# Weight splits, transposes and a third unit's values moved in the attention parts of a two-layer decoder trunk

## The chip, the cores and the metric

One Trainium2 chip, one core. The metric is device time in microseconds (us) of one execution; the kernel before takes 1085.67 us, the median of three runs (1085.3 to 1085.98).

## The reference

Two layers over 256 tokens of width 1024. Each layer is a half-step feed-forward block, a token mixer, a cross attention over 256 memory rows, and a second half-step feed-forward block, each between two root-mean-square normalisations:

```
for l in range(2):
    x = x + 0.5 * rmsnorm(swiglu(rmsnorm(x, g0), ffn[l, 0]), g1)
    h = rmsnorm(x, g2)
    if l == 0:   # four heads of causal attention (MLA) beside four heads of mLSTM
        y = concat(mla(h), mlstm(h)) @ ab_w_out
    else:        # sparse attention, keys chosen by an indexer
        y = dsa(h) @ c_w_out
    x = x + rmsnorm(y, g3)
    x = x + rmsnorm(cross_attention(rmsnorm(x, g4), rmsnorm(mem)), g5)
    x = x + 0.5 * rmsnorm(swiglu(rmsnorm(x, g6), ffn[l, 1]), g7)
```

The mLSTM part of the first mixer takes queries, keys and values of four heads, gates `li` and `lf = log_sigmoid(f)`, and works in two chunks of 128 tokens. Within a chunk the decay matrix is `cumsum(lf)` differences plus `li` under a causal mask; `sc = q k^T * exp(dmat - m)`; the first chunk's state is `sum(exp(g - m_new) k v)`; the numerator over the denominator is then normalised over each head's 128 values, multiplied by a gain, added to a skip term and gated with `sigmoid(og)`.

## The kernel before

It is written engine by engine, each with its own list of instructions in a fixed order, and semaphores between them. There is no planner: the order of each list is the schedule, and an instruction that waits holds everything behind it on its engine.

**Weights.** All large weights come as chunks of 1 MB (128 x 2048 fp32). SyncE loads a chunk into one of two or three raw slots. ScalarE writes its rounded half into a ring of four (`hi_half`, line 1656, "the high split"); VectorE writes the remainder (`lo_half`, line 2322, "the low split"); then the raw slot is free for the next load. Chunks for the memory keys and values (names `xk`, `xv`) are scaled by a gain on the way, in eight pieces (lines 1652 and 2316). TensorE forms each product from three terms, high x high, high x low, low x high. `split_to(c)` on either engine means: do your half of all chunks up to `c`, here. The chunks of the first mixer's output projection are `abo.0` to `abo.3`. `hi_half` and `lo_half` take the chunks strictly in order.

**PSUM.** Four banks rotate among all intermediate results in one fixed list (`bank_uses`): a result takes a bank when the result four places ahead in the list has been read (`take`). The other four banks hold the output rows `y`.

**First mixer, the order on TensorE.** mLSTM queries and keys (`mq`, `mk`), transposed values (`vmT`), transposed rotary parts (`rT`), the gate product `gT` (line 1427), attention scores of units 0 and 1 (lines 1267 and 1270), `gates`, the transposed keys `ktok`, half of the output gate's projection `og.0` (lines 784 to 786), transposed probabilities `pT0`, `pT1`, the running sum `cum` of the log gates (line 1298), scores 2 and 3, the decay rows `arow.0` and `arow.1`, `og.1`, `pv0`, `pv1` (attention times values, line 1289), the mLSTM scores `S.0`, `S.1`, `pT2`, `pT3`, `state.0`, `state.1`, `pv2`, `pv3`, transposed scaled scores `scT.0`, `scT.1`, `qc`, the numerators `num`, output rows from `abo.0` and half of `abo.1` (line 1076), the transposed normalised heads `hnT.0`, `hnT.1` (line 1153), and the rest of the output rows.

**First mixer, VectorE and ScalarE.** VectorE makes masked scores and row maxima (lines 2559 and 2562), ScalarE the exponentials (line 1824), VectorE the normalised probabilities (line 2574). VectorE scales the skip term `xcT` (line 2168), makes `lf` (line 2170), reads the decay rows (line 2189), reduces them (line 2191), subtracts the row maxima (line 2200), evacuates attention outputs (`output_lo`, line 2583, after ScalarE's `output_hi`, line 1839), forms the exponents `ex` (lines 2212 to 2214) that ScalarE exponentiates at line 2010, and scales the scores into `sc` (line 2219), each followed by a small copy (line 2222) that releases TensorE. The normalised heads are scaled by one operation (line 2261), behind a power on GpSimd (line 727).

**Cross attention** (`cross`, layers 0 and 1). It has four units of scores, `u0` to `u3`. After `pT` of `u2` TensorE computes output rows of token tile 0 from two chunks (24 matmuls, line 1076; `last_downs_0`), whose end is awaited by ScalarE's `square_half(s, last, 0, 0)` (line 1678). Then come `pT` of `u3`, values of `u2` and of `u3`, and output rows of token tile 1 (line 1061), which wait until VectorE has written the low halves of `u2` and `u3` (line 2583). The next chunk after `xo`, `last + 1`, is a memory chunk in layer 0 and the feed-forward chunk `G7.0` in layer 1; the dictionary `FILL` tells which: it has an entry for the stage after the first cross attention and none for the stage after the second.

Of the kernel before, what the change touches and what calls it, by code (L numbers as in the profile page):

```python
# [151 lines left out]
def bank_uses():  # L152
# [14 lines left out]
    def cross(l, s):  # L167
# [12 lines left out]
          "mq.0 mq.1 mk.0 mk.1 vmT.0 vmT.1 rT.0 rT.1 gT score0 score1 gates ktok og.0 pT0 pT1 cum "  # L180
# [37 lines left out]
def build(nc, A, out):  # L218
    ctx = ExitStack()
    with ctx:  # L220
# [140 lines left out]
        split_hi = sem("split_hi")  # L361
        split_lo = sem("split_lo")
# [41 lines left out]
        kw_done, sc_done = sem("kw_done"), sem("sc_done")  # L404
# [337 lines left out]
        def _(pe):  # L742
# [558 lines left out]
            def cross(l, s):  # L1301
# [118 lines left out]
            for name in ("mq.0", "mq.1", "mk.0", "mk.1", "vmT.0", "vmT.1"):  # L1420
                ready(name)
# [17 lines left out]
            transposes("ktok", [mkT[:, h, 0:P] for h in range(4)])  # L1439
# [190 lines left out]
        def _(act):  # L1630
# [28 lines left out]
            def split_to(c):  # L1659

                while nxt[0] <= min(c, len(chunks) - 1):
                    if chunks[nxt[0]][2]:
                        hi_half(nxt[0])
                    nxt[0] += 1

# [188 lines left out]
            def cross(l, s):  # L1854
# [134 lines left out]
            evacuate("ktok", ktok.rearrange("p h n -> p (h n)"))  # L1989
# [46 lines left out]
            ins.then_inc(dev_done, 1)  # L2036
            split_to(C["abo.3"])
# [106 lines left out]
        def mlstm_and_mla(dve, link, split_to, lo_part, row_max, normalise, output_lo):  # L2144
# [21 lines left out]
            dve.wait_ge(*freed["ktok"])  # L2166
# [16 lines left out]
            for t in range(NT):  # L2183
                name = f"arow.{t}"
                dve.wait_ge(*full(name))
                row = bank(name).rearrange("p (h n) -> p h n", h=4)
                if t == 0:
                    link(nc.vector.tensor_reduce(w0, row, AX.X, ALU.max))
# [110 lines left out]
        def _(dve):  # L2299
# [286 lines left out]
            def cross(l, s):  # L2586
# [24 lines left out]
                if s + 1 in FILL:  # L2611
                    lo_half(c, j0=5)
                    nxt[0] = c + 1
# [263 lines left out]
```

## Time and profile before

| | us |
|---|---|
| median of three runs | 1085.67 |
| the profiled execution | 1085.41 |
| its span | 1083.7 |
| TensorE busy | 1070.7 |
| VectorE busy | 776.0 |
| ScalarE busy | 564.6 |

The profile's page gives the busy time of each engine, a line of 40 slices, the chain of work that ended last and the costliest groups of instructions. The trace is read further by views of a stretch: the waits of an engine, and the instructions of an engine in order of time. Starts are in us from the start of the span; a matmul's end is modelled, so that starts of successive matmuls tell more than their lengths.

### The profile page before, as it was taken

The page shows a single profiled execution, that of the slowest core. Times are in us where ns is not written, and L with a number is a line of the kernel's source. Part 1 is how long each engine was busy: PE and PEld are TensorE (multiplying, and loading weights), DVE is VectorE, ACT ScalarE, POOL GpSimd, SP SyncE. Part 2 cuts the span into 40 slices and gives each one's busy share as a digit, 9 for nine tenths or more (in the row PEclk, how much of TensorE's full clock was granted, in tenths as well). Part 3 has the DMA queues.
Part 4 walks back from the last instruction along what each step waited for, and adds up shares of the span by engine and source line. Part 5 has one row for each costly group of instructions (what it writes and reads, how often), then busy time and mean ns, then how long its engine had stood idle before and what let it go on. Part 6 is the DMA issues. An engine that isn't in the chain of part 4 may idle for free.

```text
span 1083.7 us, 16043 instructions
## 1 busy us (share of the span) xinstructions
PE 1070.7 (99%) x6172; PEld 938.9 (87%) x6172; DVE 776.0 (72%) x1015; ACT 564.6 (52%) x816; POOL 67.8 (6%) x169
## 2 busy tenths in 40 slices
PE   8999999999999999999999999999999999999997
PEld 7888888998889888888888888888978989888886
DVE  5966769875886786676778667678487768676675
ACT  6534446667766753443465344345466666443442
POOL 3000010110020200000010000002100101000000
PEclk9999999999999999999999999999999999999999
DMA  8756474564144365644536564453804435745641
GB/s 322 249 192 222 165 273 132 170 205 151 50 184 152 108 247 199 228 166 183 194 108 246 209 233 159 190 194 108 272 14 143 175 117 195 252 159 191 222 165 40
DMA packets 50155, 194.59 MB, mean 180 GB/s; under 512 B 4496, under 2 KB 24480, under 8 KB 31792
## 3 DMA queue, kind: packets, MB, share of 16 engines
q1 hardware_dynamic: 48832, 189.54, 49.2%
q0 software_dynamic: 1264, 4.25, 1.4%
q8 instruction: 38, 0.62, 0.2%
q14 instruction: 21, 0.17, 0.0%
HBM read 192.73 MB, written 1.05 MB: 179 GB/s over the span
## 4 chain that ended last, share of the span: by engine, by line
PE 91%; DVE 5%; ACT 2%; issue 1%; DMA 1%; POOL 0%; SPq 0%; POOLq 0%; ACTq 0%; DVEq 0%
PE psum L960 21%; PE psum L1076 21%; PE psum L968 11%; PE psum L941 5%; PE psum L1061 3%; PE psum L1298 3%; PE psum L946 3%; PE psum L784 2%; PE psum L786 2%; PE psum L785 2%; PE psum L980 1%; PE psum L1267 1%; PE psum L1168 1%; PE psum L810 1%; PE psum L811 1%; PE psum L809 1%
## 5 line engine op out<-in xcount | busy, mean ns | idle before, releaser
L2322 DVE TENSOR_TENSOR w_ring<-raw,w_ring 128x2048 fp32r<-128x2048 f32 (+2 forms) x120 | 272.8, 2273 | 25.4 <-ACT w_ring L1656 25.1
L1656 ACT ACTIVATE w_ring<-raw 128x2048 fp32r<-128x2048 f32 x121 | 230.7, 1907 | 47.3 <-DMA raw<-in_ffn_w_gate 25.3
L2439 DVE TENSOR_REDUCE work<-psum 128x256 f32<-128x512 f32 x172 | 114.4, 687 | 175.3 <-PE psum L968 161.2
L960 PE MATMUL psum<-h_both,w_ring 128*128 128x512 f32 x1024 | 237.3, 389 | 0.0
L960 PEld LDWEIGHTS psum<-h_both,w_ring 128*128 128x128 f32 x1024 | 192.2, 188 | 39.9
L1076 PE MATMUL psum<-w_ring,g_both 128*128 128x512 f32 x936 | 220.0, 390 | 0.0
L1076 PEld LDWEIGHTS psum<-w_ring,g_both 128*128 128x128 f32 x936 | 173.2, 188 | 34.3
L1754 ACT ACTIVATE V<-work 128x512 f32<-128x512 f32 x44 | 27.9, 634 | 249.3 <-DVE work L2448 249.3
L968 PEld LDWEIGHTS psum<-h_both,w_ring 128*128 128x128 f32 x1024 | 127.1, 192 | 2.5
L968 PE MATMUL psum<-h_both,w_ring 128*128 128x256 f32 x1024 | 127.9, 283 | 0.0
L2322 DVE TENSOR_TENSOR w_ring<-QT,w_ring 128x2048 fp32r<-128x2048 f32 x40 | 91.4, 2285 | 2.4 <-ACT w_ring L1656 2.4
L1656 ACT ACTIVATE w_ring<-QT 128x2048 fp32r<-128x2048 f32 x40 | 76.2, 1905 | 1.9 <-DMA QT<-in_ffn_w_down 1.9
L1758 ACT ACTIVATE g_both<-V 128x512 fp32r<-128x512 f32 x43 | 27.2, 633 | 73.7 <-DVE V L2455 73.7
L941 PE MATMUL psum<-h_both,w_ring 128*128 128x512 f32 x240 | 57.7, 393 | 0.0
L941 PEld LDWEIGHTS psum<-h_both,w_ring 128*128 128x128 f32 x240 | 44.3, 188 | 8.8
L784 PE MATMUL psum<-h_both,w_ring 128*128 128x256 f32 x128 | 36.6, 286 | 0.9 <-DVE work L2559 0.9
L1688 ACT ACTIVATE h_both<-psum,gcol 128x128 fp32r<-128x128 f32 x112 | 30.8, 385 | 12.0 <-PE psum L1168 12.0
L786 PE MATMUL psum<-h_both,w_ring 128*128 128x256 f32 x128 | 36.2, 283 | 0.0
L785 PE MATMUL psum<-h_both,w_ring 128*128 128x256 f32 x128 | 36.2, 283 | 0.0
L1076 PE MATMUL psum<-w_ring,h_both 128*128 128x512 f32 x144 | 34.9, 396 | 0.0
L2455 DVE TENSOR_TENSOR V<-V,work 128x512 f32<-128x512 f32 x43 | 29.8, 692 | 6.3 <-ACT V L1754 2.8
L2354 DVE SCALAR_TENSOR_TENSOR h_both<-psum,gcol,h_both 128x128 fp32r<-128x128 f32 x112 | 30.3, 343 | 4.6 <-ACT h_both L1688 4.0
(336 smaller groups left out, 1560.7 us busy)
## 6 DMA issues: line engine op xcount, KB each, us to landing
raw<-in_ffn_w_gate SPq DMA_DIRECT2D x43, 1024.0 KB, 4.8
raw<-in_ffn_w_up SPq DMA_DIRECT2D x43, 1024.0 KB, 4.8
QT<-in_ffn_w_down SPq DMA_DIRECT2D x40, 1024.0 KB, 4.8
raw<-in_ab_w_in SPq DMA_DIRECT2D x7, 1024.0 KB, 5.5
gain_row<-in_norm_g POOLq DMA_DIRECT2D x8, 512.0 KB, 6.6
raw<-in_ffn_w_down SPq DMA_DIRECT2D x4, 1024.0 KB, 4.7
raw<-in_xa_wk SPq DMA_DIRECT2D x4, 1024.0 KB, 4.8
raw<-in_ab_w_out SPq DMA_DIRECT2D x4, 1024.0 KB, 5.0
```

Source lines behind the costliest of these rows:

```text
L784: nc.tensor.matmul(o, wh, a_hi[:, k, :], start=(k == 0), stop=False)
L785: nc.tensor.matmul(o, wh, a_lo[:, k, :], start=False, stop=False)
L786: last = nc.tensor.matmul(o, wl, a_hi[:, k, :], start=False, stop=(k == KT - 1))
L941: nc.tensor.matmul(outs[j][:, :], hi[:, k, P * j:P * (j + 1)], h_both[:, k].rearrange("p a n -> p (a n)"), start=(k == 0), stop=False)
L946: last = nc.tensor.matmul(outs[j][:, 0:TOK], lo[:, k, P * j:P * (j + 1)], h_hi[:, k, :], start=False, stop=(k == KT - 1))
L960: nc.tensor.matmul(outs[-1][:, :], hi[:, k, P * j:P * (j + 1)], h_both[:, k].rearrange("p a n -> p (a n)"), start=(k == 0), stop=False)
L968: last = nc.tensor.matmul(outs[2 * n + j][:, 0:TOK], lo[:, k, P * j:P * (j + 1)], h_hi[:, k, :], start=False, stop=(k == KT - 1))
L1061: last = nc.tensor.matmul(psum[:, 2 * t + half, :], a, w[:, k, 512 * half:512 * (half + 1)], start=(first and k == 0 and a is ah and w is hi),
L1076: last = nc.tensor.matmul(psum[:, 2 * t + half, :], a, w[:, k, 512 * half:512 * (half + 1)], start=(first and k == 0 and a is ah and w is hi),
L1656: nc.scalar.activation(w_hi[:, c % RING, 0:k * n], raw_at(c)[:, 0:k * n], ACT.Copy)\
L2322: nc.vector.tensor_tensor(w_lo[:, c % RING, 0:k * n], raw_at(c)[:, 0:k * n], w_hi[:, c % RING, 0:k * n].bitcast(F32), ALU.subtract).then_i ...
L2439: nc.vector.tensor_reduce(dst[:, p % 2, TOK * j:TOK * (j + 1)], bank(name).rearrange("p (a n) -> p n a", a=2), AX.X, ALU.add)\
```

## The change

It moves instructions within the lists of the engines and cuts two into parts; nothing that is computed changes.

1. First mixer: `ktok` goes ahead of `gT` in the bank list, on TensorE and on ScalarE, and the high split of `abo.0` goes behind `gT` on ScalarE. The low split of `abo.0` goes on VectorE from ahead of the row maxima of units 0 and 1 to behind their normalisations.
2. VectorE reads the second decay row right after the first one is finished.
3. VectorE scales the scores ahead of the exponents `ex`, and the two small copies go away; TensorE waits for the scaling itself.
4. ScalarE takes the squares of the deviations ahead of the sigmoid; VectorE scales the normalised heads in two halves.
5. Both cross attentions: `pT` of `u3` and the values of `u2` go inside the last half of the output rows of tile 0. In the first one the next chunk's splits are cut in two; in the second ScalarE's high split of the next chunk goes behind the copy of `pT` of `u3`.

```diff
 # bank list
-          "mq.0 mq.1 mk.0 mk.1 vmT.0 vmT.1 rT.0 rT.1 gT score0 score1 gates ktok og.0 pT0 pT1 cum "
+          "mq.0 mq.1 mk.0 mk.1 vmT.0 vmT.1 rT.0 rT.1 ktok gT score0 score1 gates og.0 pT0 pT1 cum "
 # TensorE, cross
-                last_downs_0(pair, True, ready=lambda: ready(f"pv{u1}"))
-                prob_transposes(u3)
-                values(u2)
+                def third_values():
+                    prob_transposes(u3)
+                    values(u2)
+                last_downs_0(pair, True, ready=lambda: ready(f"pv{u1}"), between=third_values)
                 values(u3)
 # TensorE, first mixer
-            for name in ("mq.0", "mq.1", "mk.0", "mk.1", "vmT.0", "vmT.1"):
+            ready("mk.0")
+            ready("mk.1")
+            transposes("ktok", [mkT[:, h, 0:P] for h in range(4)])
+            for name in ("mq.0", "mq.1", "vmT.0", "vmT.1"):
                 ready(name)
...
-            transposes("ktok", [mkT[:, h, 0:P] for h in range(4)])
             feature_major("og.0", h_hi, h_lo)
...
-                pe.wait_ge(sc_done, t + 1)
+                ready(f"S.{t}")
...
-            pe.wait_ge(hn_done, 1)
             for i in range(2):
+                pe.wait_ge(hn_done, i + 1)
                 transposes(f"hnT.{i}", [hh[:, 4 * t + 2 * i + j, :] for j in range(2) for t in range(NT)])
 # ScalarE, cross (memory_hi: the scaled high split, four of its eight pieces)
                 exps(u3)
-                split_to(C[f"xo{l}.1"] + 1)
+                last = C[f"xo{l}.1"]
+                if s + 1 in FILL:
+                    memory_hi(last + 1, 0)
                 prob_copy(u3)
-                last = C[f"xo{l}.1"]
+                if s + 1 in FILL:
+                    memory_hi(last + 1, 1)
+                    nxt[0] = last + 2
+                else:
+                    split_to(last + 1)
                 square_half(s, last, 0, 0)
 # ScalarE, first mixer
+            evacuate("ktok", ktok.rearrange("p h n -> p (h n)"))
+            evacuate("gT", gT, bank("gT")[:, 0:TOK])
             split_to(C["abo.0"])
-            evacuate("gT", gT, bank("gT")[:, 0:TOK])
             exps(0)
...
-            evacuate("ktok", ktok.rearrange("p h n -> p (h n)"))
...
-            act.wait_ge(*freed["og.1"])
-            og = ogT[:, :, :].rearrange("p h n -> p (h n)")
-            nc.scalar.activation(og, og, ACT.Sigmoid).then_inc(og_done, 1)
             act.wait_ge(mean_done, 1)
             for g in range(8):
                 ...
             ins.then_inc(dev_done, 1)
+            (the three lines of the sigmoid)
 # VectorE, first mixer
-            split_to(C["abo.0"])        (ahead of row_max(0))
             normalise(0)
             normalise(1)
-            dve.wait_ge(*freed["ktok"])
+            split_to(C["abo.0"])
+            dve.wait_ge(*freed["mk.1"])
...
                 if t == 0:
+                    dve.wait_ge(*full("arow.1"))
+                    nc.vector.tensor_tensor(Dm[:, 1], bank("arow.1")..., tri, ALU.add).then_inc(freed["arow.1"][0], 1)
                     normalise(2)
                     normalise(3)
...
-            ex = ...                    (three instructions, ex_in)
             for t in range(NT):
                 ...
                 nc.vector.scalar_tensor_tensor(sc[:, t], ...).then_inc(freed[name][0], 1)
-                dve.wait_ge(*freed[name])
-                nc.vector.tensor_copy(sm[:, 20, 0:1], a_[:, 0, 0:1]).then_inc(sc_done, 1)
+            ex = ...                    (three instructions, ex_in)
             split_to(C["abo.1"])
...
-            nc.vector.tensor_tensor(hh, hh, groups(sm[:, 15, :]), ALU.mult).then_inc(hn_done, 1)
+            for i in range(2):
+                (half i of hh, the same product).then_inc(hn_done, 1)
 # VectorE, cross
                 if s + 1 in FILL:
-                    lo_half(c, j1=5)
+                    lo_half(c, j1=4)
                 else:
                     split_to(c)
                 output_lo(u2)
+                output_lo(u3)
                 if s + 1 in FILL:
-                    lo_half(c, j0=5)
+                    lo_half(c, j0=4)
                     nxt[0] = c + 1
-                output_lo(u3)
```

## Rows read from the trace of the kernel before

**Rows 1.** The page, busy time of each engine over the span.
```profile
PE 1070.7 (99%) x6172; PEld 938.9 (87%) x6172; DVE 776.0 (72%) x1015; ACT 564.6 (52%) x816; POOL 67.8 (6%) x169
```
**Rows 2.** TensorE in order of time: start, us, what, count, idle before.
```profile
260.75 0.63 PE L1153 MATMUL psum<-ident,KTs 128*128 128x128 f32 x4
262.29 0.36 PE L784 MATMUL psum<-h_both,w_ring 128*128 128x256 f32 x1 [0.90 <-DVE work L2559]
...
268.55 0.51 PE L1298 MATMUL psum<-small,upper 128*128 128x4 f32 x4
```
**Rows 3.** ScalarE in order of time, 259 to 263 us.
```profile
259.34 0.42 ACT L1669 ACTIVATE lat<-psum 128x256 f32<-128x256 f32 x1
259.78 1.28 ACT L1824 ACT_TABLE_LOAD   x1
262.63 0.41 ACT L1824 ACTIVATE work<-work,nmax 128x128 f32<-128x128 f32 x1 [1.57 <-DVE nmax L2562]
```
**Rows 4.** VectorE in order of time, 264 to 268 us.
```profile
264.53 0.42 DVE L2574 TENSOR_TENSOR work<-work,einv 128x256 f32<-128x256 f32 x1
266.43 1.14 DVE L2168 TENSOR_SCALAR shared<-shared,pcol 128x256 f32<-128x256 f32 x4 [1.48 <-ACT xmT L1669]
267.49 0.16 DVE L2170 SCALAR_TENSOR_TENSOR small<-gts,small 128x8 f32<-128x8 f32 x1
```
**Rows 5.** VectorE in order of time, 279 to 284 us.
```profile
279.87 0.68 DVE L2189 TENSOR_TENSOR latT<-psum,cmask 128x512 f32<-128x512 f32 x1
280.58 0.69 DVE L2191 TENSOR_REDUCE small<-latT 128x4 f32<-128x512 f32 x1
...
282.77 0.15 DVE L2212 TENSOR_TENSOR small<-small 128x4 f32<-128x4 f32 x1
...
283.12 0.69 DVE L2219 SCALAR_TENSOR_TENSOR lat<-psum,latT 128x512 f32<-128x512 f32 x1
```
**Rows 6.** ScalarE in order of time, 283 to 287 us.
```profile
283.25 0.21 ACT L2010 ACTIVATE small<-small 128x12 f32<-128x12 f32 x1 [0.39 <-DVE small L2214]
...
284.32 1.91 ACT L1656 ACTIVATE w_ring<-raw 128x2048 fp32r<-128x2048 f32 x1
```
**Rows 7.** TensorE in order of time, the transposes of the scaled scores and of the heads.
```profile
283.96 1.43 PE L1298 MATMUL psum<-vaug,xmT 128*128 128x130 f32 x8 [0.22 <-DVE lat L2219]
...
287.01 1.04 PE L1153 MATMUL psum<-ident,lat 128*128 128x128 f32 x8
...
299.38 1.09 PE L1153 MATMUL psum<-ident,lat 128*128 128x128 f32 x8 [0.45 <-DVE lat L2261]
```
**Rows 8.** VectorE in order of time, 298 us.
```profile
298.09 1.23 DVE L2261 TENSOR_TENSOR lat<-lat,small 128x1024 f32<-128x1024 f32 x1
```
**Rows 9.** TensorE in order of time, first cross attention.
```profile
360.54 4.55 PE L1061 MATMUL psum<-w_ring,h_both 128*128 128x512 f32 x18 [0.44 <-DVE h_both L2583]
```
**Rows 10.** TensorE in order of time, second cross attention.
```profile
877.10 5.72 PE L1076 MATMUL psum<-w_ring,h_both 128*128 128x512 f32 x24
882.66 0.60 PE L1153 MATMUL psum<-ident,work 128*128 128x128 f32 x4
883.10 2.01 PE L1289 MATMUL psum<-work,XV 128*128 128x128 f32 x16
885.26 4.38 PE L1061 MATMUL psum<-w_ring,h_both 128*128 128x512 f32 x18 [0.15 <-DVE h_both L2583]
```
**Rows 11.** ScalarE in order of time, second cross attention.
```profile
879.78 1.91 ACT L1656 ACTIVATE w_ring<-raw 128x2048 fp32r<-128x2048 f32 x1
883.30 0.60 ACT L1669 ACTIVATE work<-psum 128x512 f32<-128x512 f32 x1 [1.60 <-PE psum L1153]
883.79 0.59 ACT L1678 ACTIVATE V<-psum 128x512 f32<-128x512 f32 x1
```
**Rows 12.** VectorE in order of time, second cross attention.
```profile
881.73 2.29 DVE L2322 TENSOR_TENSOR w_ring<-raw,w_ring 128x2048 fp32r<-128x2048 f32 x1 [0.91 <-ACT w_ring L1656]
884.78 0.42 DVE L2583 TENSOR_TENSOR h_both<-psum,h_both 128x256 fp32r<-128x256 f32 x1 [0.76 <-ACT h_both L1839]
```

More of the change, by code:

```diff
@@ L361, in build @@
         split_hi = sem("split_hi")
+        memory_hi_half = sem("memory_hi_half")
         split_lo = sem("split_lo")
@@ L403, in build @@
         key_decay_in, key_decay_done = sem("key_decay_in"), sem("key_decay_done")
-        kw_done, sc_done = sem("kw_done"), sem("sc_done")
+        kw_done = sem("kw_done")
         qc_scaled = sem("qc_scaled")
@@ L1664, in split_to, with memory_hi @@
                     nxt[0] += 1
+            def memory_hi(c, half):
+                k, n = size(c)
+                if half == 0:
+                    act.wait_ge(*landed(c))
+                    act.wait_ge(*used(c - RING))
+                for j in range(4 * half, 4 * half + 4):
+                    o = slice(n * j, n * (j + 1))
+                    ins = nc.scalar.activation(w_hi[:, c % RING, o], raw_at(c)[:, o], ACT.Copy,
+                                               scale=mem_gain(chunks[c][0], j))
+                ins.then_inc(split_hi if half else memory_hi_half, 1)
             def evacuate(name, dst, src=None, func=ACT.Copy, scale=1.0):
@@ L2036, in _ @@
             ins.then_inc(dev_done, 1)
+            act.wait_ge(*freed["og.1"])
+            og = ogT[:, :, :].rearrange("p h n -> p (h n)")
+            nc.scalar.activation(og, og, ACT.Sigmoid).then_inc(og_done, 1)
             split_to(C["abo.3"])
@@ L2184, in mlstm_and_mla @@
                 name = f"arow.{t}"
-                dve.wait_ge(*full(name))
-                row = bank(name).rearrange("p (h n) -> p h n", h=4)
                 if t == 0:
+                    dve.wait_ge(*full(name))
+                    row = bank(name).rearrange("p (h n) -> p h n", h=4)
                     link(nc.vector.tensor_reduce(w0, row, AX.X, ALU.max))
-                nc.vector.tensor_tensor(Dm[:, t], row, tri, ALU.add).then_inc(freed[name][0], 1)
+                    nc.vector.tensor_tensor(Dm[:, t], row, tri, ALU.add).then_inc(freed[name][0], 1)
                 dve.wait_ge(*freed[name])
@@ L2201, in mlstm_and_mla @@
                 if t == 0:
+                    dve.wait_ge(*full("arow.1"))
+                    nc.vector.tensor_tensor(Dm[:, 1], bank("arow.1").rearrange("p (h n) -> p h n", h=4), tri, ALU.add)                        .then_inc(freed["arow.1"][0], 1)
                     normalise(2)
@@ L2209, in mlstm_and_mla @@
             output_lo(1)
-            ex = sm[:, 16:18, :]
-            nc.vector.tensor_tensor(ex[:, 0, 4:8], mnew, mj[:, 1, :], ALU.subtract)
-            link(nc.vector.tensor_tensor(ex[:, 1, :].rearrange("p (t n) -> p t n", t=NT), bc, mj, ALU.add))
-            nc.vector.tensor_scalar(ex[:, 1, :], ex[:, 1, :], -1.0, None, ALU.mult).then_inc(ex_in, 1)
             for t in range(NT):
@@ L2220, in mlstm_and_mla @@
                                                Dm[:, t], ALU.mult, ALU.mult).then_inc(freed[name][0], 1)
-                dve.wait_ge(*freed[name])
-                nc.vector.tensor_copy(sm[:, 20, 0:1], a_[:, 0, 0:1]).then_inc(sc_done, 1)
+            ex = sm[:, 16:18, :]
+            nc.vector.tensor_tensor(ex[:, 0, 4:8], mnew, mj[:, 1, :], ALU.subtract)
+            link(nc.vector.tensor_tensor(ex[:, 1, :].rearrange("p (t n) -> p t n", t=NT), bc, mj, ALU.add))
+            nc.vector.tensor_scalar(ex[:, 1, :], ex[:, 1, :], -1.0, None, ALU.mult).then_inc(ex_in, 1)
             split_to(C["abo.1"])
@@ L2260, in mlstm_and_mla @@
             link(nc.vector.tensor_tensor(sm[:, 15, :], sm[:, 15, :], den, ALU.mult))
-            nc.vector.tensor_tensor(hh, hh, groups(sm[:, 15, :]), ALU.mult).then_inc(hn_done, 1)
+            for i in range(2):
+                o = hh.rearrange("p (t g) n -> p t g n", t=NT)[:, :, 2 * i:2 * i + 2, :]
+                scale = sm[:, 15, :].rearrange("p (t g) -> p t g", t=NT)[:, :, 2 * i:2 * i + 2]
+                nc.vector.tensor_tensor(o, o, scale.unsqueeze(3).to_broadcast([P, NT, 2, HD]), ALU.mult)                    .then_inc(hn_done, 1)
             dve.wait_ge(og_done, 1)
```

3 lines of the change are left out of this document (1 added, 2 removed).

## The prediction

> **What bounds the kernel now.** I read the page first: TensorE is busy for 1070.7 us of a span of 1083.7, VectorE for 776.0 [rows 1]. So the time can change only where TensorE stands still, or comes to stand still; the change alters none of its products. The view of TensorE's waits says where it stands still near the edits, and the view in order of time says for whom. The reader is to see five places. Ahead of `og.0` it waits 0.90 us for VectorE's first masked score, whose bank `og.0` takes [rows 2]. Ahead of `state.0` it waits 0.22 us for the scaled scores, ahead of `hnT.0` 0.45 us for the scaled heads [rows 7]. Ahead of the output rows of tile 1 it waits 0.44 us in the first cross attention and 0.15 us in the second, each time for the low half of a unit's output [rows 9, 10]. These are 2.16 us, plus the transposes of `ktok` that could slip into another gap. Everything behind them is a chain of full TensorE work, so that what TensorE gains or loses at a place reaches the end, unless a later wait eats it. Clock and DMA stay out of this: no wait near the edits names a DMA as its releaser.
>
> **First mixer, up to `cum`: -0.6 us.** With `ktok` moved up, `og.0` takes the bank of `gT`, free long before. Its transposes start at 260.75 [rows 2] and are gone from here, so `og.0` starts at about 260.85 in place of 262.29: 1.4 us won. The four transposes (0.44 us, 882.66 to 883.10 in rows 10, the same kind) now stand ahead of `gT`, where TensorE waits for ScalarE's copies of the values anyway; they cost about 0.1 us. The next thing in TensorE's list that can be late is `cum`, which needs `lf` from VectorE. On ScalarE the high split of `abo.0` now follows the copy of `gT`. That copy stands at 259.34 only because the split is ahead of it [rows 3]; `gT` itself is complete about 2 us before the gates product that precedes 260.75, so at 258.7 (estimate). Copy 0.4, split 1.91 less 0.1 of overlap [rows 6], so the table load goes from 259.78 to 260.9 and ends at 262.2: the exponentials start 0.45 us earlier than 262.63 [rows 3]. On VectorE the last normalisation then starts at 264.05 (264.53 before) and ends at 264.5 [rows 4]. Behind it now comes the low split, 2.29 us [rows 12], to 266.7; then the four scalings, which before had waited 1.48 us for ScalarE and so had room [rows 4], 1.06 us to 267.7; then `lf`, done at 267.85, where before it was done at 267.65. TensorE, 1.4 us early, would reach `cum` at 267.15 (268.55 before [rows 2]) and waits until 267.95. Of 1.4 us, 0.6 are left. The bounds are 1.4 (if `lf` were in time) and 0.
>
> **From `cum` to the numerators: all of it lost, 0.2 us more.** VectorE works without a pause from the row maxima of unit 2 to the first `output_lo`; reading the second decay row earlier moves work inside this stretch and takes nothing out but one wait. What such a wait costs: line 2191 starts 0.03 us after the end of line 2189, whose result it awaits [rows 5], whereas `lf` starts 0.08 us before the scaling ends [rows 4]; so 0.1 us. VectorE is then 0.7 us early. The wait of `S.0` for the bank of `arow.1` goes, but TensorE meets `output_lo` a few transposes on and waits there.
>
> The Trainium skill (VectorE: DVE Perf Modes, The DRAIN you can't avoid) says that a semaphore between two vector operations costs nothing extra, since the next one waits for the pipe to empty either way. The rows just named disagree by 0.1 us. By the page VectorE would be 0.6 us early here and the sum 0.1 us higher.
>
> Now the scores. Their first scaling starts 0.7 us before the place of line 2212 at 282.77 [rows 5], at 282.07, is done at 282.76 in place of 283.81, and `state.0` can start at 282.9 in place of 283.96 [rows 7]. The second follows at 282.7 and ends at 283.35. Only then come the three exponent operations, whose first started at 282.77 and whose last released ScalarE just before 283.25 [rows 5, 6]: 0.44 us. So ScalarE gets its exponents at 283.75, 0.5 us later than now. It stood idle for them already, 0.39 us [rows 6], so it has no slack. Queued behind that wait in ScalarE's list are the copies of `pT2` and `pT3`, the high split of `abo.2` (1.91 us from 284.32 [rows 6]), the copies of the states behind it, two output copies, and the copies of the transposed scores. All start 0.5 us later. TensorE, which needs the copy of `pT2`, gets to values 2 only 0.7 us early, and the transposes of the scaled scores need the bank of `state.0`, whose copy now begins at 284.8 + 1.91 - 0.1 = 286.6 and ends at about 287.0: they start at 287.0, as now (287.01 [rows 7]). Then `qc` awaits the output copies, and the numerators come about 0.2 us later than now (estimate: 0.5 us of delay less the slack of 0.3 us that the copies gain where they had waited for TensorE). Bounds: 0.4 late, or up to 0.7 us early if the copies are not what ends last; I take 0.2 late, by the rows.
>
> **The heads: -0.55 us.** The scaling of 1024 columns takes 1.23 us from 298.09 [rows 8]. Half of it is an operation of 512 columns, 0.69 us (line 2219, rows 5). `hnT.0` can start 0.54 us earlier, the second half is ready 0.1 us after the whole was. The chain from `hnT.0` through gating to the output rows goes on in step, and it is this chain that sets the residual. TensorE has output rows to compute until shortly before, so of its wait of 0.45 us [rows 7] little more can be won at once, but the later short waits in the same chain go too. The sigmoid behind the squares frees nothing: the variance waits on VectorE behind the low split of `abo.2`, not for the squares; and the sigmoid has 3 us until it is used. The first mixer: +0.2 - 0.55 = -0.35 us, bounds -1.5 and +0.4.
>
> **First cross attention: -0.1 us.** `pT3` and values 2 go inside the output rows, so unit 2 is complete early and VectorE no longer holds it behind five pieces of the split. But ScalarE's list has the square of tile 0's first half ahead of unit 2's output copy, and that square awaits the end of these output rows, now later by four transposes and eight value matmuls, 0.44 + 0.9 us. Unit 2's low half comes 0.1 us later than now, unit 3's right behind it, which removes a second short wait. Bounds: -0.44, the whole wait [rows 9], and +0.5.
>
> **Second cross attention: +1.8 us.** No memory chunk follows here, so the branch without `FILL` applies: ScalarE copies `pT3` first and splits `G7.0` behind it; VectorE's list still has the low split ahead of both `output_lo`. Before, the split filled a hole: ScalarE had it from 879.78 to 881.69 and then stood idle 1.60 us until `pT3` [rows 11]. After: 24 output matmuls take 5.56 us (877.10 to 882.66 [rows 10]), 0.232 each; `pT3` comes after 18, at 881.27; ScalarE's copy starts 0.64 us behind it, as before (882.66 to 883.30), at 881.91; the high split 0.49 us behind (883.30 to 883.79 [rows 11]), at 882.40, and ends at 884.31 (before 881.69). VectorE's low split starts 0.04 us behind that, as before, at 884.35, lasts 2.29 us, and `output_lo` of unit 2 can start 0.08 us before its end, at 886.56 (884.78 before [rows 12]). TensorE followed that by 0.48 us (885.26), so it starts on tile 1 at 887.04: 1.8 us later. TensorE's wait there is then 2 us in place of 0.15 [rows 10]. Nothing behind gives it back: the last feed-forward block is full TensorE work. Bounds: +1.2, if TensorE's own list is slower than I have it, and +2.2, a full high split of 1.91 and some.
>
> **Sum.** -0.35 - 0.1 + 1.8 = +1.35 us. The profiled execution took 1085.41 us, 0.26 less than the median: 1086.8 by it, 1087.0 by the median; I say 1086.9.
>
> **The rivals.**
> *The mixer turns to a loss.* `lf` now has a low split of 2.29 us and the scalings ahead of it. If the exponentials are not 0.45 us earlier but later, say because the split holds the table load longer, `lf` slips by the same amount; from 0.6 us of slip on, TensorE reaches `cum` no earlier than now, ScalarE's delay by the exponents then comes undiminished (+0.8 at the numerators, +0.3 after the heads), and each further 0.1 us counts whole. With 0.4 us more: +0.7 - 0.1 + 1.8 = +2.4, 1087.9. For it: VectorE was idle for `ktok` only 1.48 us there [rows 4], less than the split. Against it: ScalarE's order can be followed row by row. Chance 0.13.
> *The mixer keeps what it removes.* All waits of TensorE there go, 1.4 at `og.0`, 0.2 at `state.0`, 0.3 at the heads: -1.9 - 0.1 + 1.8 = -0.2, 1085.3. The Trainium skill (Perfetto Trace Analysis, Optimization Strategy) advises just this, to find the gaps on the contended engine and make the dependency that ends them start sooner. Against it: the dependency that is next, `lf`, lies within 0.8 us, and the exponents come later by 0.5. Chance 0.14.
> *The second cross attention does not pay.* If low split and output copy were not in VectorE's order as I read them, the term of +1.8 would be near 0: 1085.1 with my mixer, and 1083.5 with the mixer in full. Against it: list order is binding. Chance 0.07.
>
> **How the numbers follow.** The forecast has 0.66 and its own range is 1086.2 to 1087.6. The range of 8 in 10 reaches to the edges of the rivals, 1085.3 to 1088.1. A change of 0.2% is 2.2 us, about what a measurement of this kernel can tell from none. Below 1083.5 needs the third rival and more: 0.05. Above 1087.84 needs the first rival: 0.14. Between: 0.81.
>
> **What would show it.** `og.0` starting near 260.9 and `cum` waiting for line 2170; ScalarE's line 2010 half a microsecond later than 283.25 although VectorE's scores are earlier; the numerators not earlier than now; `hnT.0` 0.3 us or more earlier. In the second cross attention a wait of TensorE of about 2 us for line 2583 ahead of line 1061, with ScalarE's split of `G7.0` behind the copy of `pT3`. I am wrong if that wait is under 1 us, or if the mixer's end moves by more than 1 us.

## The result, and the profile after

The changed kernel takes 1088.87 us (median of 8 runs, 1087.36 to 1090.76); the kernel before, run beside it on the same chip, 1085.83 us (8 runs, 1085.24 to 1086.63). The ratio is 1.0028, with a 95% interval of 1.0019 to 1.0037: 3.0 us slower. The forecast was 1086.9 us, with a range of 1085.3 to 1088.1. The sign and the place were right, the size was too small: 1.2 us over the 1085.67 of its time, where 3.0 came. The profiled execution took 1088.85 us with a span of 1087.1 us: 3.44 more than the one before.

**Where the time went.** Everything ahead of the second cross attention's output rows nets to nothing: their first product of tile 0 starts at 877.11, before at 877.10 [rows 10]. Here is TensorE in order of time from there (start, us, engine, line, what, count, and in brackets the idle time before it with its releaser):
```profile
877.11 4.36 PE L1077 MATMUL psum<-w_ring,h_both 128*128 128x512 f32 x18
881.31 0.60 PE L1154 MATMUL psum<-ident,work 128*128 128x128 f32 x4
881.74 1.06 PE L1290 MATMUL psum<-work,XV 128*128 128x128 f32 x8
882.55 1.64 PE L1077 MATMUL psum<-w_ring,h_both 128*128 128x512 f32 x6
884.03 1.05 PE L1290 MATMUL psum<-work,XV 128*128 128x128 f32 x8
887.06 5.99 PE L1062 MATMUL psum<-w_ring,h_both 128*128 128x512 f32 x18 [1.98 <-DVE h_both L2611]
892.88 0.82 PE L1169 MATMUL psum<-ident,x_state 128*128 128x128 f32 x6
```
Tile 1 starts at 887.06 in place of 885.26 [rows 10]: +1.80, the forecast's 887.04. But the 18 products there then take 5.82 us up to the next transposes. Before, it was 4.21 us; its row for those transposes:
```profile
889.47 1.03 PE L1168 MATMUL psum<-ident,x_state 128*128 128x128 f32 x8
```
So the delay grows from 1.80 to 3.41 us behind the wait. The reason stands in the view of short stretches of the changed kernel (stretch, its length, busy time and count of TensorE, its weight loads, VectorE, ScalarE and GpSimd, then the granted clock, the DMA share and GB/s):
```profile
885.00:887.00 2.00, 0.08 (x1) 0.00 (x0) 2.00 (x3) 2.00 (x5) 1.88 (x2) 1.00 0.00 0
887.00:888.00 1.00, 0.94 (x4) 0.82 (x5) 1.00 (x4) 0.88 (x1) 0.65 (x2) 1.00 0.41 66
888.00:889.00 1.00, 1.00 (x4) 0.71 (x3) 0.96 (x2) 0.00 (x0) 0.00 (x0) 0.50 0.73 238
889.00:890.00 1.00, 1.00 (x4) 0.80 (x3) 0.98 (x2) 0.00 (x0) 0.00 (x0) 0.50 1.10 467
890.00:891.00 1.00, 1.00 (x4) 0.81 (x3) 0.00 (x0) 0.00 (x0) 0.00 (x0) 0.50 0.67 279
891.00:892.00 1.00, 1.00 (x5) 0.79 (x5) 0.00 (x0) 0.30 (x1) 0.00 (x0) 0.80 0.00 0
```
TensorE was idle for nearly all of 885 to 887, and about a microsecond after it had started again the granted clock fell to 0.50, that is 1.2 of 2.4 GHz, until some way into 891. In a stretch of 1 us at 1.00 this view counts six products (those on an edge in both stretches); here it counts four. The Trainium skill (TensorE: Matmul & The Clock Gate, HAM oscillation) says that a wait of TensorE in the middle of a kernel can bring the clock down and that the work behind it then starts cold; this trace agrees: 1.6 us are lost behind a wait of 1.98. Two other traces with the same wait, of experiments 2 and 10, do not show the fall.

**The chain of that wait**, ScalarE and then VectorE of the changed kernel:
```profile
881.94 0.60 ACT L1687 ACTIVATE work<-psum 128x512 f32<-128x512 f32 x1 [2.05 <-PE psum L1154]
882.44 1.91 ACT L1662 ACTIVATE w_ring<-raw 128x2048 fp32r<-128x2048 f32 x1
```
```profile
884.38 2.29 DVE L2350 TENSOR_TENSOR w_ring<-raw,w_ring 128x2048 fp32r<-128x2048 f32 x1 [3.56 <-ACT w_ring L1662]
886.58 0.75 DVE L2611 TENSOR_TENSOR h_both<-psum,h_both 128x256 fp32r<-128x256 f32 x2
```
Against [rows 11, 12]: ScalarE stands idle for 2.05 us where it had split, the high split starts at 882.44 instead of 879.78, the low split at 884.38 instead of 881.73, and the output of unit 2 is written at 886.58 instead of 884.78. The forecast had 882.40, 884.35 and 886.56.

**The mixer.** The longest waits of TensorE from 256 to 318 us in the changed kernel (engine, tile and line, waited for; total, times, longest):
```profile
PE psum L1299 <- DVE small L2195: 0.6, 1, 0.6
PE psum L1154 <- ACT KTs L1687: 0.5, 1, 0.5
PE psum L1290 <- ACT work L1687: 0.5, 1, 0.5
PE psum L1154 <- DVE h_both L2611: 0.4, 1, 0.4
```
None of the old ones at `og.0`, `state.0` and `hnT.0` [rows 2, 7] is left; four new ones hold 2.0 us: `cum`, `pv2`, `scT.0`, and `pT2` for the output of unit 0. TensorE's rows for `og.0`, `cum`, `state.0`, `pv2`, `scT.0` and `hnT.0`:
```profile
261.05 0.37 PE L785 MATMUL psum<-h_both,w_ring 128*128 128x256 f32 x1
...
268.12 0.61 PE L1299 MATMUL psum<-small,upper 128*128 128x4 f32 x4 [0.63 <-DVE small L2195]
...
283.14 1.22 PE L1299 MATMUL psum<-vaug,xmT 128*128 128x130 f32 x8
284.82 2.02 PE L1290 MATMUL psum<-work,V 128*128 128x128 f32 x16 [0.46 <-ACT work L1687]
287.38 1.06 PE L1154 MATMUL psum<-ident,lat 128*128 128x128 f32 x8 [0.54 <-ACT KTs L1687]
...
299.42 1.25 PE L1154 MATMUL psum<-ident,lat 128*128 128x128 f32 x8
```
Against [rows 2, 7]: -1.24, -0.43, -0.82, then +0.37 and +0.04. From the transposed values, where the mixer begins, the way to `hnT.0` is 44.33 us (299.42 less 255.09 below), before it was 44.44 (299.38 less 254.94):
```profile
255.09 1.04 PE L1154 MATMUL psum<-ident,vaug 128*128 128x128 f32 x8
```
```profile
254.94 1.04 PE L1153 MATMUL psum<-ident,vaug 128*128 128x128 f32 x8
```
By these two traces the mixer is worth 0.1 us. Eight traces have this mixer, and the way is 44.33 to 44.43 us in seven of them and 44.71 in that of experiment 4; in the three with the old one it is 44.41 to 44.44.

### The profile page after: what moved, and what is told of

The parts are those of the page before. It is cut to its first block, busy times and chain, and to the rows that moved or that the text cites. A ratio compares the mean times of both kernels' runs of the same rounds, so it can differ in the third digit from the quotient of the medians.

```text
span 1087.1 us, 16043 instructions
## 1 busy us (share of the span) xinstructions
PE 1073.3 (99%) x6172; PEld 940.5 (87%) x6172; DVE 775.4 (71%) x1014; ACT 564.8 (52%) x816; POOL 70.1 (6%) x169
## 4 chain that ended last, share of the span: by engine, by line
PE 90%; DVE 5%; ACT 2%; DMA 1%; issue 1%; POOL 0%; SPq 0%; POOLq 0%; ACTq 0%; DVEq 0%
PE psum L1077 22%; PE psum L961 21%; PE psum L969 11%; PE psum L942 4%; PE psum L1062 3%; PE psum L1299 3%; PE psum L947 2%; PE psum L785 2%; PE psum L786 1%; PE psum L787 1%; PE psum L981 1%; PE psum L1268 1%; PE psum L1154 1%; PE psum L1169 1%; PE psum L811 1%
## 5 line engine op out<-in xcount | busy, mean ns | idle before, releaser
L1696 ACT ACTIVATE V<-psum 128x512 f32<-128x512 f32 x32 | 19.2, 599 | 30.0 <-PE psum L1077 18.1
```

## The experiments

Each was timed in rounds beside the kernel before, whose medians in the four sets of runs were 1086.04 (1 to 4), 1086.01 (5 to 8), 1086.08 (9 and 10) and 1086.07 (11 and 12). From the transposes of unit 3 to tile 1 the changed kernel takes 5.75 us (881.31 to 887.06); where a wait is compared, this way is given.

**1. ScalarE's split ahead of the copy again.** In `cross`, on ScalarE, second cross attention only:
```diff
                 if s + 1 in FILL:
                     memory_hi(last + 1, 0)
+                else:
+                    split_to(last + 1)
                 prob_copy(u3)
...
-                else:
-                    split_to(last + 1)
```


> The changed kernel with one step undone: in the second cross attention ScalarE makes the high split of G7.0 ahead of the copy of pT3 again; all else as changed. Theory A: the late split makes TensorE wait 2.0 us, and this wait in turn brings the granted clock from 2.4 down to 1.2 GHz for the output rows behind it (it was 0.50 from 888 to 891 us). Then both go: the wait ahead of line 1062 falls under 0.8 us, the clock stays at 1.00, and the time is that of the kernel before within 0.5 us (1085.8 to 1086.1). Rival B: the clock falls for a cause outside TensorE's wait (the load of 1 MB and VectorE's work that lie there). Then only the 1.8 us of the wait go, the clock still falls somewhere from 885 to 892 us, and the time is about 1087.3. Rival C: the loss sits in the first mixer or the first cross attention: over 1087.5.

1086.25 us (1085.46 to 1087.87, 11 runs), ratio 1.0000 (0.9990 to 1.0009). TensorE:
```profile
878.53 4.37 PE L1077 MATMUL psum<-w_ring,h_both 128*128 128x512 f32 x18
882.73 0.60 PE L1154 MATMUL psum<-ident,work 128*128 128x128 f32 x4
...
887.12 4.38 PE L1062 MATMUL psum<-w_ring,h_both 128*128 128x512 f32 x18 [0.62 <-DVE h_both L2611]
891.34 1.03 PE L1169 MATMUL psum<-ident,x_state 128*128 128x128 f32 x8
```
The way is 4.39 us, the wait 0.62, and the 18 products take 4.22. One placement on one engine carries the loss of 3 us, and the rest of the change is neutral within the interval, 1 us either way. From tile 0's first product to tile 1 it is 8.59 us here (878.53 to 887.12), 9.95 in the changed kernel and 8.16 before [rows 10], so that 0.43 us of the delay are left; experiment 7 shows what holds them.

**2. The second cross attention's part alone**, in the kernel before:
```diff
-                last_downs_0(pair, True, ready=lambda: ready(f"pv{u1}"))
-                prob_transposes(u3)
-                values(u2)
+                def third_values():
+                    prob_transposes(u3)
+                    values(u2)
+
+                last_downs_0(pair, True, ready=lambda: ready(f"pv{u1}"), between=third_values if l else None)
+                if not l:
+                    third_values()
...
+                if not l:
+                    split_to(C[f"xo{l}.1"] + 1)
+                prob_copy(u3)
                 split_to(C[f"xo{l}.1"] + 1)
-                prob_copy(u3)
```


> The kernel before with the changes of the second cross attention alone (pT3 and values 2 inside the output rows of tile 0, high split of G7.0 behind the copy of pT3). Theory A: the whole loss of the change comes back: a wait of 2.0 us ahead of the output rows of tile 1, most executions with a stretch at half clock behind it, 1088.5 to 1089. Rival B (the clock falls for another cause that the kernel before does not have): 1087.6, no stretch at half clock. Rival C (mixer or first cross attention): under 1087.

1089.93 us (1087.38 to 1091.06, 6 runs), ratio 1.0030 (1.0018 to 1.0042). The profiled execution was the quickest of the six, and shows why: the wait is there, the fall of the clock is not.
```profile
887.20 4.38 PE L1061 MATMUL psum<-w_ring,h_both 128*128 128x512 f32 x18 [1.98 <-DVE h_both L2589]
891.41 1.03 PE L1168 MATMUL psum<-ident,x_state 128*128 128x128 f32 x8
```
```profile
888.00:889.00 1.00, 1.00 (x6) 0.83 (x5) 0.96 (x3) 0.02 (x1) 0.00 (x0) 1.00 0.70 229
```
18 products in 4.21 us at a clock of 1.00: with the same wait of 1.98 us the clock falls in some executions and not in others. Experiment 10 shows the same for the changed kernel itself.

**3. The wait filled.** TensorE gets 16 transposes of a constant, which nobody reads, behind `values(u3)` of the second cross attention:
```diff
                 values(u3)
+                if l:
+                    for _ in range(16):
+                        nc.tensor.transpose(psum[:, 3, 0:P], ident[:, :], ident[:, :])
                 ready(f"pv{u2}")
```


> The changed kernel with 16 transposes of the unit matrix added on TensorE ahead of its wait in the second cross attention, into a PSUM bank that is free there; nothing reads them. They take 16 x 0.11 = 1.75 us of the wait of 1.98 us, so the output rows start no later than in the changed kernel. Theory A: the wait as such stays (rows of tile 1 start at 887.1), but TensorE is not idle, the clock stays at 1.00, and the time is 1.8 us above before, 1087.5, about 1.5 under the changed kernel. Rival B: the fall of the clock does not hang on TensorE's idleness: still 0.50 for some 3 us, 1088.9.

1087.35 us (1086.59 to 1089.60, 11 runs), ratio 1.0009 (1.0000 to 1.0018), 1.3 above the kernel before, where the changed kernel is 3.0 above it, with the same delay of tile 1:
```profile
883.68 0.60 PE L1154 MATMUL psum<-ident,work 128*128 128x128 f32 x4
...
887.28 1.91 PE L1343 MATMUL psum<-ident 128*128 128x128 f32 x16
889.44 3.93 PE L1062 MATMUL psum<-w_ring,h_both 128*128 128x512 f32 x16 [0.25 <-DVE h_both L2614]
```
The way is 5.76 us, as in the changed kernel, and the clock stays at 1.00. As unfilled waits are not always followed by a fall, this one trace proves little; what counts is the mean over all filled executions, taken below.

**4. VectorE's low split behind both outputs.**
```diff
                     lo_half(c, j1=4)
-                else:
-                    split_to(c)
                 output_lo(u2)
                 output_lo(u3)
                 if s + 1 in FILL:
                     lo_half(c, j0=4)
                     nxt[0] = c + 1
+                else:
+                    split_to(c)
```


> The changed kernel with VectorE's low split of G7.0 behind both output_lo of the second cross attention; ScalarE's high split stays behind the copy of pT3. Theory A: unit 2's low half then waits only for ScalarE (split to 884.3, square to 885.0, copy to 885.2), TensorE starts tile 1 near 885.8, 0.5 us later than before, with a wait of 0.7 us; a wait so short does not bring the clock down: 1086.3 to 1086.6. If instead the high split on ScalarE were what costs, and not the low split behind it: over 1087.5.

1086.63 us (1085.86 to 1088.66, 11 runs), ratio 1.0004 (0.9995 to 1.0013):
```profile
881.75 0.60 PE L1154 MATMUL psum<-ident,work 128*128 128x128 f32 x4
...
886.15 4.38 PE L1062 MATMUL psum<-w_ring,h_both 128*128 128x512 f32 x18 [0.64 <-DVE h_both L2611]
```
The way is 4.40 us and the wait 0.64. ScalarE's order, left here as the change has it, costs TensorE only through the low split.

**5. The exponents later on ScalarE.** To experiment 1, ScalarE's wait for the exponents and their exponential move behind `output_hi(3)`; a wait for the exponential is added where ScalarE first uses it, ahead of scaling `qc`:
```diff
-            act.wait_ge(ex_in, 1)
-            nc.scalar.activation(... ACT.Exp).then_inc(ex_done, 1)
             prob_copy(2)
             prob_copy(3)
...
             output_hi(3)
+            act.wait_ge(ex_in, 1)
+            nc.scalar.activation(... ACT.Exp).then_inc(ex_done, 1)
...
+            act.wait_ge(ex_done, 1)
```


> The kernel of the run with ScalarE's split of G7.0 ahead again (e1), and in the first mixer ScalarE's wait for the exponents and their exponential moved from ahead of the copies of pT2 and pT3 to behind the output copies of units 2 and 3. Theory A: ScalarE's wait for the exponents, 1.58 us in the changed kernel, is what ate the mixer's gain. Without it TensorE loses the waits of 0.5 us ahead of values 2 and of 0.5 us ahead of the transposes of the scaled scores, and hnT.0 comes about 1.1 us earlier, counted from the transposes of the mLSTM values: mixer -1.0, time 1085.0, if nothing later takes it. Rival B: the path through VectorE (low split of abo.2 behind the heads, POOL's power) has other work ahead, so that hnT.0 moves by less than 0.4 us; time 1085.8.

1085.32 us (1083.72 to 1088.60, 12 runs), ratio 0.9996 (0.9986 to 1.0006): by the time alone no difference from the kernel before can be told, and the gain is read from the way. The mixer's way to `hnT.0` is 43.15 us (254.71 to 297.86) in place of 44.33. Where the changed kernel's ScalarE waits for the exponents (first fence) this one copies the probabilities (second fence), and both waits of TensorE for its copies, ahead of `pv2` and `scT.0`, are gone:
```profile
283.98 0.21 ACT L2034 ACTIVATE small<-small 128x12 f32<-128x12 f32 x1 [1.58 <-DVE small L2247]
284.10 1.07 ACT L1687 ACTIVATE work<-psum 128x512 f32<-128x512 f32 x2
```
```profile
282.51 1.09 ACT L1687 ACTIVATE work<-psum 128x512 f32<-128x512 f32 x2 [0.48 <-PE psum L1154]
```

**6. The gates ahead of the low split.** To experiment 5, VectorE's `split_to("abo.0")` moves from behind `normalise(1)` to behind `lf`:
```diff
             normalise(1)
-            split_to(C["abo.0"])
             dve.wait_ge(*freed["mk.1"])
...
                 ALU.min, ALU.subtract).then_inc(lf_done, 1)
+            split_to(C["abo.0"])
```


> e5, and VectorE's low split of abo.0 behind lf in place of ahead of the skip scalings. Theory A: the wait of 0.6 us ahead of cum goes (lf is done near 265.9, before TensorE gets there), and everything to hnT.0 comes 0.4 to 0.6 us earlier still: 0.5 us under e5. Rival B: the low split now stands in front of VectorE's reading of cum and of the row maxima; then cum starts earlier but score maxima do not, and hnT.0 gains less than 0.2 us against e5.

1083.93 us (1083.38 to 1084.89, 11 runs), ratio 0.9981 (0.9972 to 0.9990). The way to `hnT.0` is 42.23 us (254.66 to 296.89): 0.92 less again, more than expected. VectorE:
```profile
264.23 1.13 DVE L2193 TENSOR_SCALAR shared<-shared,pcol 128x256 f32<-128x256 f32 x4
265.30 0.17 DVE L2195 SCALAR_TENSOR_TENSOR small<-gts,small 128x8 f32<-128x8 f32 x1
265.39 2.28 DVE L2351 TENSOR_TENSOR w_ring<-raw,w_ring 128x2048 fp32r<-128x2048 f32 x1
```
`lf` is done well before `cum` asks for it, and the split fits into the time in which VectorE waits for `cum` and for the next scores. By the medians it is 1.4 us under experiment 5, more than the way explains. Part of that is scatter: none of the 22 executions of experiments 6 and 7 lies more than 1.5 us above its kernel's median, while 10 of the 35 of the kernel before beside them took over 1087 us; no run shows why.

**7. Unit 2's output ahead of the square**, on ScalarE in both cross attentions, to experiment 6:
```diff
+                output_hi(u2)
                 square_half(s, last, 0, 0)
-                output_hi(u2)
                 output_hi(u3)
```


> e6, and in both cross attentions ScalarE copies unit 2's output ahead of the square of tile 0's first half. Unit 2's values are complete 1.4 us before the output rows that the square awaits. Theory A: TensorE's waits of 0.6 us ahead of the output rows of tile 1 go in both (under 0.1 each): -0.6 in the first, -0.6 in the second, together 1.1 us under e6, and with the mixer's gain 1083.5 to 1084.3, the fastest so far. Rival B: the residual of tile 0, which comes later by the copy, takes the place: the waits go but TensorE waits as long ahead of the turned rows (line 1169).

1083.48 us (1082.33 to 1084.97, 11 runs), ratio 0.9972 (0.9964 to 0.9981): the quickest kernel here, 2.5 us below the kernel before. By the median it is 0.45 us under experiment 6, where 1.1 had been expected, and the two intervals overlap. No wait stands ahead of tile 1 any more (879.85 to 883.37, a way of 3.52 us), but part comes back at the transposes that follow in the first cross attention:
```profile
358.50 4.37 PE L1062 MATMUL psum<-w_ring,h_both 128*128 128x512 f32 x18
363.17 1.10 PE L1169 MATMUL psum<-ident,x_state 128*128 128x128 f32 x6 [0.30 <-DVE x_state L2407]
```

**8. The mixer alone**, both cross attentions as before on all engines:
```diff
-                last_downs_0(pair, True, ready=lambda: ready(f"pv{u1}"), between=third_values)
+                last_downs_0(pair, True, ready=lambda: ready(f"pv{u1}"))
+                prob_transposes(u3)
+                values(u2)
...
+                split_to(C[f"xo{l}.1"] + 1)
                 prob_copy(u3)
...
-                    lo_half(c, j1=4)
+                    lo_half(c, j1=5)
```

> The changed kernel with both cross attentions as before, so the first mixer's part alone. The traces of before and after put it at 0.0 to +0.1 us at the mixer's end (my forecast had said -0.35). Theory A: ratio to before 1.000 within 0.0005, no added stretch at half clock, 1085.7 to 1086.2. Rival: a loss of the mixer hidden in the spread: over 1086.6.

1086.11 us (1084.42 to 1088.00, 11 runs), ratio 1.0001 (0.9992 to 1.0009); the way to `hnT.0` is 44.34 us (257.10 to 301.44). The mixer's edits together are worth 0.1 us by the way; by the time they can't be told from nothing, within 1 us.

**9. Experiment 2 with the 16 transposes** of experiment 3, by the same edit.

> The kernel of e2 (the second cross attention's change alone) with the 16 unread transposes ahead of TensorE's wait, as in e3. Theory A: without the idle stretch the clock stays; the time is the 1.8 us of the late output rows above before, 1087.6 to 1088.0, and at least 1.5 us under a median of e2 taken anew. Rival B (the fall does not hang on idleness): within 0.5 us of e2, 1089.5 or more.

1088.50 us (1086.42 to 1089.92, 12 runs), ratio 1.0021 (1.0012 to 1.0029): over the 1087.6 to 1088.0 expected, in two clusters (five at 1086.4 to 1087.5, seven at 1088.3 to 1089.9). It lies 1.4 us under experiment 2, which was not taken again beside it. So the expectation missed, and experiments 10 to 12 ask what the clusters are.

**10. The changed kernel again**, with no edit.

> The changed kernel itself, again, on the chip of the run beside it. Theory A: +2.8 to +3.5 us over before, single executions in two groups, near +1.5 (no fall of the clock behind the wait) and near +3 (with it). Rival: the +3.0 of the first comparison was drawn high by its eight executions; about +1.5.

1088.62 us (1087.13 to 1091.23, 10 runs), ratio 1.0023 (1.0014 to 1.0033): +2.5 us, just under what was expected. Its profiled execution, at 1087.13, shows a wait of 2.0 us ahead of tile 1 again and a clock of 1.00 behind it:
```profile
888.00:889.00 1.00, 1.00 (x6) 0.83 (x5) 0.96 (x2) 0.00 (x0) 0.00 (x0) 1.00 0.70 254
```

**11. The wait filled with products**, 8 of 512 columns instead of 16 transposes, in case the transposes did not hold the clock:
```diff
+                if l:
+                    (c0, a_hi0, _), _ = pair
+                    hi0 = w_hi[:, c0 % RING, 0:512]
+                    for _ in range(8):
+                        nc.tensor.matmul(psum[:, 3, :], a_hi0[:, 0, 0:P], hi0, start=True, stop=True)
```


> The changed kernel, with the wait filled by 8 products of 512 columns of the kind of the output rows (8 x 0.23 = 1.8 us, into a free bank, first product of the output rows of tile 0 repeated; nothing reads them) in place of transposes. Where the transposes of e3 and e9 left the clock to fall in some executions (8 of 23 were over 1088, against 19 of 24 unfilled), Theory A2: it hangs on how much the array does, and transposes count for less than products. Then here hardly any execution is over 1088.2 beyond the share that before has, median 1087.4 to 1087.7, ratio 1.0015. Rival: what is left over 1088 in the filled kernels has another cause, that products do not remove: a third of the executions over 1088 again.

1087.63 us (1087.26 to 1089.73, 11 runs), ratio 1.0014 (1.0006 to 1.0023).

**12. Experiment 3 again**, beside experiment 11.

> The kernel of e3 again, on the same chip as e11, so that the two kinds of filling can be held side by side. Theory A2: between e11 and the changed kernel (1088.7), with two groups of executions, near 1087.3 and near 1089; share over 1088 a third. Rival (no difference between the kinds): equal to e11 within 0.3 us.

1088.05 us (1086.39 to 1089.74, 12 runs), ratio 1.0015 (1.0006 to 1.0025): six of 12 near 1087, six near 1089. Products leave a cluster near 1089 too (four of 11), so nothing here speaks for a difference between the two fillers.

**What the clusters are.** Experiment 3's profiled execution took 1089.60, experiment 12's, the same kernel, 1086.69, and both have a clock of 1.00 behind the filled wait. Their difference of 2.91 us arises before the mixer: the transposed values start at 257.28 in the one and at 254.32 in the other, 2.96 apart.
```profile
257.28 1.04 PE L1154 MATMUL psum<-ident,vaug 128*128 128x128 f32 x8
```
```profile
254.32 1.04 PE L1154 MATMUL psum<-ident,vaug 128*128 128x128 f32 x8
```
A wait with a fallen clock behind it stands here too, in the first 20 us, which no edit touches. TensorE's wait for the first weight chunks and then the short stretches, of experiment 3 and then of experiment 12:
```profile
PE psum L904 <- ACT w_ring L1924: 2.0, 1, 2.0
```
```profile
0.00:10.00 10.00, 6.21 (x27) 5.60 (x27) 3.17 (x8) 5.00 (x11) 1.34 (x9) 0.99 0.77 278
10.00:20.00 10.00, 10.00 (x49) 8.63 (x48) 8.60 (x11) 7.88 (x12) 1.29 (x2) 0.84 0.97 379
```
```profile
PE psum L904 <- ACT w_ring L1924: 0.2, 1, 0.2
```
```profile
0.00:10.00 10.00, 8.07 (x36) 7.22 (x37) 5.02 (x12) 6.71 (x14) 1.35 (x9) 1.00 0.82 266
10.00:20.00 10.00, 10.00 (x57) 8.71 (x56) 8.13 (x10) 6.76 (x9) 2.19 (x5) 1.00 1.02 424
```
The wait of 2.0 us is followed by a clock of 0.84 over ten microseconds, in which 1.6 of them are lost (0.16 of ten), and it is itself 1.8 us longer. These 3.4 us are a little more than the difference; where the rest is made up was not followed. Over all 14 profiled executions, that early wait was 1.9, 2.0 and 2.5 us in three (experiments 1, 3 and 8), each with a fallen clock behind it, and at most 1.7 in the others, which have 1.00 there. What makes the first chunks late in some executions was not tried.

The kernel before scatters in the same way (115 runs in five sets, 1084.64 to 1089.36), and means over many executions average over it. Above the mean of these 115 (1086.30) the filled kernels lie by 1.76 us with transposes (35 runs) and by 1.81 with products (11): the 1.8 us of the delay and no more. The unfilled ones (24 runs) lie 2.67 above it. Set by set, over the kernel before beside them, the unfilled are 3.0, 3.3 and 2.5 us higher on the mean, the filled 1.5, 2.1, 1.6 and 1.7; over 1088 us took 19 of the 24 unfilled executions and 19 of the 46 filled. So an idle wait costs 0.9 us on the mean beyond its length, with a standard error of 0.3, and the only such cost that a trace shows is the clock. At 1.6 us each time, as in the one trace that has it, the clock fell in a little over half of the executions (an estimate, with an error of about 0.2 in that share). Of the three profiles of unfilled kernels one shows the fall.

## Why the prediction was wrong

**The step that failed** is "Clock and DMA stay out of this: no wait near the edits names a DMA as its releaser". The reason given is one for DMA alone; nothing was asked of the clock, though the same text put a wait of 2 us on an engine that is busy for 99% of the span. The sum has no term for what a wait does to the work behind it: 1.6 us in the profiled execution. Between the two profiled executions tile 0's first product of the second cross attention is 0.01 us later (877.11 for 877.10), and 0.01 + 1.80 + 1.61 = +3.42, against 3.44. Without that term the time is inside the range, and executions without a fall came out there: 1087.13 and 1087.38 (the profiles of experiments 10 and 2). With the same delay and no idle wait the mean loses the surplus (experiments 3, 9, 11 and 12: 1.77 us in place of 2.67), so the term hangs on TensorE's idleness and not on the delay.

A smaller part of the miss is in the other terms: up to the second cross attention -0.45 us was forecast, and +0.01 came, of which 0.15 are from the start (255.09 for 254.94). And the median of the eight executions, +3.0, lies above the mean of all 24 with that wait, +2.7. Neither sign of being wrong that the prediction named appeared; times above 1087.84 were given to the first rival alone, and came without it.

**Second cross attention: right in mechanism and size.** +1.8 forecast, +1.80 measured, with each start between within 0.04 us. Experiments 1 and 4 cut the chain at either engine and bring the way from 5.75 down to 4.4 us.

**Mixer up to `cum`: right.** `lf` is the next thing late. Less the 0.15 us from the start, `og.0` is 1.39 us earlier for the 1.4 forecast and `cum` 0.58 for 0.6, behind a wait of 0.63 us for `lf`. Experiment 6 confirms the low split of 2.28 us as its cause.

**From `cum` to the numerators: right in mechanism, mis-sized by 0.2.** ScalarE's exponents come 0.73 us later than before (283.98 for 283.25 [rows 6]), 0.58 without the start, for the 0.5 forecast, and TensorE meets it twice, at `pv2` and at `scT.0`. The numerators, forecast 0.2 late, come 0.58 late (289.36 for 288.78), 0.43 without the start. The 0.3 us of slack that the copies were to make up were an estimate without a row: before, an output copy had waited for TensorE for 0.15 us (at 287.21), and 0.15 were made up. Experiment 5 gives 1.18 us back by moving the exponential.

**The heads: right.** From the numerators (+0.58) to `hnT.0` (+0.04) 0.54 us are won, for 0.55 forecast. The mixer as a whole brought 0.1 for 0.35, and the difference is that of the numerators.

**First cross attention: sign wrong, size small.** The wait ahead of tile 1 is 0.62 us in place of 0.44 [rows 9]:
```profile
360.81 4.38 PE L1062 MATMUL psum<-w_ring,h_both 128*128 128x512 f32 x18 [0.62 <-DVE h_both L2611]
```
Tile 1 starts at 360.81 in place of 360.54, +0.27, from a common start (the transposes of unit 2 stand at 351.83 and 351.82); -0.1 had been forecast. Behind its 18 products +0.10 is left (365.03 for 364.93). The square ahead of unit 2's output was named as what holds it, and experiment 7 confirms that.

**The rivals.** That the mixer keeps what it removes is refuted by its four new waits. That it turns to a loss would have given a time nearer to the result (1087.9) for a wrong reason: experiment 8 shows no such loss. That the second cross attention doesn't pay is refuted by experiment 2.

## What to carry to other kernels

On an engine that is nearly always busy, price a new wait twice: its length, and a chance of half a clock behind it. A wait of 2.0 us brought a further 1.6 us in part of the executions, waits of 0.6 us in none of the traces. An instruction that waits should stand as late in its engine's list as its reader allows: here an exponential moved behind six copies and a weight split gained 1.2 us, a weight split behind a gate 0.9, both by the way to `hnT.0`, and a split put behind a waiting copy lost 3 by the time. When two profiles differ by a few microseconds, compare the ways between fixed places, and only then the spans.

## What the runs showed of the hardware

- The granted clock went from 1.00 to 0.50 behind a wait of 1.98 us on TensorE, about 1 us after work had resumed, and was back at 1.00 by 892; in two other executions with the same wait it never fell. Behind the three early waits of 1.9 to 2.5 us it fell too, behind the eleven of up to 1.7 us it did not.
- With 16 unread transposes or 8 unread products in the wait it was 1.00 in every trace taken (experiments 3, 9, 11 and 12), and the mean over 46 executions lay 0.9 us below that of the 24 unfilled ones. Four traces alone would not show this, as two of three unfilled ones have 1.00 as well.
- The place where the mixer begins scatters by 3.0 us between the profiled executions (254.32 to 257.28), through an early wait and the clock behind it; so single executions say little below 2 us.
